# A hybrid encoder block on one core: the first tile's norm weights folded into its rounding, its high weight parts used first, and the last attention pair's reloads reordered

## The reference

```python
def _rmsnorm(x, g):
    y = xf * lax.rsqrt(jnp.mean(xf * xf, axis=-1, keepdims=True) + RMS_EPS)
    return (y * g)
...
h = _rmsnorm(x, norm_g)
proj = h @ w_in          # a_val, a_glu, z_a, q, k, v, z_b, g_logits
y_a = (_conv_module(a_val, a_glu, ...) * jax.nn.silu(z_a)) @ w_pw_a
attn = _neighbourhood_attention(q, k, v, rpb)   # 16 heads, 8 x 16 window, softmax
y_b = (attn * jax.nn.silu(z_b)) @ w_o_b
merged = sigmoid(g_a) * y_a + sigmoid(g_b) * y_b
out = _rmsnorm(x + merged @ w_out, final_g)
```

## Time and profile before

| | us |
|---|---|
| median of 3 runs | 1741.43 |
| lowest, highest | 1738.87, 1742.03 |
| the profiled execution's own time | 1739.94 |
| its span, first to last instruction | 1738.1 |

### The profile page before, as it was taken

How to read it: one execution, slowest core, us unless ns; L and a number is a source line. 1 busy time by engine, 2 the same in 40 slices (tenths; PEclk the granted TensorE clock), 3 DMA queues, 4 the chain that set the end, 5 groups by cost and what they waited for, 6 DMA issues and landing times.

```text
span 1738.1 us, 24594 instructions
## 1 busy us (share of the span) xinstructions
PE 1726.1 (99%) x8604; PEld 1405.8 (81%) x8604; DVE 1162.3 (67%) x1797; ACT 466.8 (27%) x925; POOL 200.2 (12%) x251
## 2 busy tenths in 40 slices
PE   9999999999999999999999999999999999999998
PEld 7888877788888888888888888888877888888886
DVE  6549255897689489579669948976985755335332
ACT  5411133123122122222222222221334344102222
POOL 1110011011011011101101100210110064000001
PEclk9999999999999999999999999999999999999999
DMA  8751345545435625634543453463467765543223
GB/s 296 244 93 49 94 110 142 157 121 158 127 86 168 169 50 145 173 84 125 167 126 97 133 164 90 121 167 111 115 171 282 256 208 175 192 133 110 74 91 127
DMA packets 299177, 247.56 MB, mean 142 GB/s; under 512 B 117815, under 2 KB 252999, under 8 KB 298988
## 3 DMA queue, kind: packets, MB, share of 16 engines
q1 hardware_dynamic: 246666, 153.04, 32.2%
q10 hardware_dynamic: 48578, 79.97, 13.3%
q0 software_dynamic: 3872, 13.75, 3.2%
HBM read 158.78 MB, written 87.90 MB: 142 GB/s over the span
## 4 chain that ended last, share of the span: by engine, by line
PE 89%; DMA 5%; DVE 2%; SPq 1%; ACT 1%; issue 1%; ACTq 0%; POOL 0%; POOLq 0%; DVEq 0%
PE pg L1523 71%; PE pg L1541 12%; PE pO L1638 3%; PE pS L1621 3%; DMA raw<-in_w_in 1%; DMA x_d<-work 1%; DMA work<-p_d 1%; DMA work<-tb_d 1%; SPq L528 1%; ACT xs L867 0%; DMA p_d<-work 0%; SPq L464 0%; DMA c_d<-work 0%; DVE work L1298 0%; ACT work L764 0%
## 5 line engine op out<-in xcount | busy, mean ns | idle before, releaser
L1523 PE MATMUL pg<-xs,ws 128*128 128x512 f32 x5688 | 1312.0, 391 | 0.8 <-DVE work L1419 0.5
L1523 PEld LDWEIGHTS pg<-xs,ws 128*128 128x128 f32 x5688 | 1062.1, 188 | 232.9 <-issue 11.4
L1214 DVE SCALAR_TENSOR_TENSOR work<-work 128x1551 f32<-128x1551 f32 x240 | 438.5, 1827 | 4.6
L1541 PE MATMUL pg<-ws,xs 128*128 128x512 f32 x1008 | 237.0, 393 | 0.7 <-DVE xs L1157 0.7
L1541 PEld LDWEIGHTS pg<-ws,xs 128*128 128x128 f32 x1008 | 190.4, 189 | 41.6 <-DVE ws L1108 1.0
L680 POOL TENSOR_TENSOR work<-work 128x384 f32<-128x384 bf16 (+1 forms) x72 | 62.3, 866 | 981.1 <-DVE small L1286 968.3
L1286 DVE CUSTOM_DVE_ANT_0 work<-pS,work 128x384 f32<-128x384 f32 (+1 forms) x192 | 88.4, 510 | 114.7 <-PE pS L1621 113.9
L955 ACT ACTIVATE work<-work,small 128x384 f32<-128x384 f32 (+1 forms) x192 | 109.2, 570 | 156.0 <-DVE small L1286 156.0
L1108 DVE TENSOR_TENSOR ws<-raw,ws 128x1024 fp32r<-128x1024 f32 x89 | 110.2, 1239 | 38.5 <-ACT ws L733 38.5
L733 ACT ACTIVATE ws<-raw 128x1024 fp32r<-128x1024 f32 x89 | 93.5, 1053 | 126.3 <-PE pg L1523 98.6
L1298 DVE STREAM_TRANSPOSE work<-work 128x384 f32<-128x384 f32 (+1 forms) x192 | 102.6, 534 | 6.6
(11 more groups left out here) (111 smaller groups left out, 905.8 us busy)
## 6 DMA issues: line engine op xcount, KB each, us to landing
raw<-in_w_in SPq DMA_DIRECT2D x70, 512.0 KB, 4.6
p_d<-work SPq DMA_DIRECT2D x256, 96.0 KB, 2.1
work<-p_d ACTq DMA_DIRECT2D x64, 384.0 KB, 5.1
work<-v_d SPq DMA_DIRECT2D x128, 96.0 KB, 2.7
p_d<-work SPq DMA_DIRECT2D x128, 64.0 KB, 1.9
work<-p_d ACTq DMA_DIRECT2D x32, 256.0 KB, 4.4
v_d<-work ACTq DMA_DIRECT2D x24, 256.0 KB, 2.1
za_d<-work ACTq DMA_DIRECT2D x24, 256.0 KB, 2.1
```

The source lines that it names most:

```text
L1214: nc.vector.scalar_tensor_tensor(cv[:, 0:CLEN], u[:, k:k + CLEN], cur[:, k:k + 1], cv[:, 0:CLEN], ALU.mult, ALU.add).then_inc(tap_ok, 1)
L1523: last = nc.tensor.matmul(pg[b][:], wt(s, wpart)[:, k * P:(k + 1) * P], xs[:, k, xpart, chunk(n)], start=(k == 0 and wpart == 1), stop=(k ...
L1541: last = nc.tensor.matmul(pg[b][:], xs[:, k, xpart, t * P:(t + 1) * P], wt(s0 + k // 2, wpart)[:, chunk(k % 2)], start=(k == 0 and xpart = ...
```

## The change

In the head the norm's weights of tile 0 are no longer multiplied into the row. PE turns them into a column by eight one-column transposes, DVE copies it to SBUF (`gcol`), and ACT's rounding and DVE's rest of tile 0 take it as a scale per partition, now in pieces of 128 columns. PE's first two groups are written out: the high weight parts of a slot are used by both parts of x before its low part is wanted, the next tile's transposes stand between, and group 1 begins before group 0 ends. Small products of the identity (`warm`) stand ahead and between the column's transposes. The rest of weight slot 0 moves from DVE to POOL. The squares of tiles 2 to 5 are placed otherwise. The broadcast of the norm's weights is issued behind weight slots 2 and 3.

In the last pair SP waits for the last probabilities before it issues tb tile 3, every tb tile has a semaphore, slot S_YB+1 is issued behind tile 6 and ahead of 0 and 1, and the refill of the first 512 tokens (and PE's first group on them) goes in the order 3, 4, 5, 2, 6, 7, 0, 1.

```diff
@@ -96,6 +96,7 @@
 EARLY = 11
+TB_ORDER = (3, 4, 5, 2, 6, 7, 0, 1)
 SHUFFLED = 5
...
@@ -448,9 +454,9 @@
             load_x(1)
-            sp.dma_start(ngb, norm_g[0:1, :].to_broadcast([P, D])).then_inc(ng_in, 16)
             for s in range(2, 4):
                 piece_s(s, w_rows(w0, C_V * P, s))
+            sp.dma_start(ngb, norm_g[0:1, :].to_broadcast([P, D])).then_inc(ng_in, 16)
             for t in range(2, 8):
...
@@ -528,12 +534,14 @@
             def load_tb(k):
-                sp.dma_start(home(k), tb_d[k]).then_inc(tbs_in, 16)
+                sp.dma_start(home(k), tb_d[k]).then_inc(tbs_in[k], 16)
             def load_tb_early():
                 sp.wait_ge(tb_out, 16 * (PAIRS - 1))
                 sp.wait_ge(qk_done, BLK * PAIRS)
+                for n in range(2):
+                    sp.wait_ge(p_in[n], 96 * PAIRS)
                 load_tb(3)
...
@@ -576,9 +584,6 @@
-            piece_y(S_YB + 1)
-            for n in range(2):
-                sp.wait_ge(p_in[n], 96 * PAIRS)
             sp.wait_ge(bias_ok, 18 * PAIRS)
...
@@ -586,6 +591,7 @@
             load_tb(6)
+            piece_y(S_YB + 1)
             sp.wait_ge(pv_done, BLOCKS * PAIRS)
...
@@ -646,11 +652,14 @@
             nc.gpsimd.memset(half, -0.5).then_inc(const_ok, 1)
-            nc.gpsimd.memset(onerow, 1.0).then_inc(const_ok, 1)
-            pool.wait_ge(const_ok, 3)
+            pool.wait_ge(const_ok, 2)
             nc.gpsimd.affine_select(out=ident[:], in_=ident[:], compare_op=ALU.not_equal, fill=1.0, base=0,
                                     pattern=[[-1, P]], channel_multiplier=1).then_inc(const_ok, 1)
             for t in range(NT):
+                if t == 1:
+                    pool.wait_ge(w_hi, 1)
+                    nc.gpsimd.tensor_tensor(wt(0, 1), raw_of(0), wt(0, 0).bitcast(F32), ALU.subtract).then_inc(w_lo, 1)
...
@@ -769,6 +778,13 @@
                     act.wait_ge(ht_ps, 2 * t + hf + 1)
+                if t == 0:
+                    act.wait_ge(gc_ok, 1)
+                    for k in range(4 * hf, 4 * hf + 4):
+                        nc.scalar.activation(xs[:, k, 0, 0:P], pH[k // 2][:, k % 2 * P:(k % 2 + 1) * P], ACT.Copy,
+                                             scale=gcol[:, k:k + 1]).then_inc(x_hi if k % 4 == 3 else x0_hi, 1)
+                    return
                 nc.scalar.activation(split_of(xs[:, 4 * hf:4 * hf + 4, 0, t * P:(t + 1) * P]), h_of(t, hf),
...
@@ -798,12 +814,19 @@
             for t in range(NT):
-                for n in range(t + (2 if t < 2 else 4), min(t + (3 if t < 1 else 5), NT)):
-                    square(n)
+                if t == 1:
+                    square(3)
+                    square(4)
+                elif t >= 2 and t + 4 < NT:
+                    square(t + 4)
                 if t + 1 < NT:
                     for hf in range(2):
                         h_hi(t + 1, hf)
+                    if t == 0:
+                        square(2)
                     take_v(t)
+                    if t == 1:
+                        square(5)
                 if t == 4:
...
@@ -857,7 +880,12 @@
                 act.wait_ge(g_done, g_next - NCH + n + 1)
-                for k in ks:
+                for k in TB_ORDER if (phase, n) == (1, 0) else ks:
+                    if phase == 1 and n == 0:
+                        if k == KT - 1:
+                            act.wait_ge(o_out, NCH * PAIRS)
+                        else:
+                            act.wait_ge(tbs_in[k], 16)
                     if phase == 2:
...
@@ -867,9 +895,6 @@
             def refill_tb(n):
-                if n == 0:
-                    act.wait_ge(tbs_in, 16 * 7)
-                    act.wait_ge(o_out, NCH * PAIRS)
                 refill_hi(1, n, lambda k: home(k)[:, chunk(n)], 1.0)
...
@@ -1128,9 +1153,8 @@
                     for hf in range(2):
-                        dve.wait_ge(ng_ps, hf + 1)
                         x = xt[:, 0, chunk(hf)]
-                        nc.vector.scalar_tensor_tensor(x, x, rstd[:, 0:1], pS[hf][:], ALU.mult, ALU.mult).then_inc(xn_ok, 1)
+                        nc.vector.tensor_scalar(x, x, rstd[:, 0:1], None, ALU.mult).then_inc(xn_ok, 1)
                     return
...
@@ -1152,16 +1176,26 @@
             def h_lo(t, hf):
+                if t == 0:
+                    for k in range(4 * hf, 4 * hf + 4):
+                        dve.wait_ge(*first_part(x_hi, x0_hi, k | 1))
+                        nc.vector.scalar_tensor_tensor(xs[:, k, 1, 0:P], pH[k // 2][:, k % 2 * P:(k % 2 + 1) * P],
+                                                       gcol[:, k:k + 1], xs[:, k, 0, 0:P].bitcast(F32), ALU.mult,
+                                                       ALU.subtract).then_inc(x_lo if k % 4 == 3 else x0_lo, 1)
+                    return
                 dve.wait_ge(x_hi, 2 * t + hf + 1)
                 rows = slice(4 * hf, 4 * hf + 4)
                 nc.vector.tensor_tensor(split_of(xs[:, rows, 1, t * P:(t + 1) * P]), h_of(t, hf),
                                         split_of(xs[:, rows, 0, t * P:(t + 1) * P].bitcast(F32)),
                                         ALU.subtract).then_inc(x_lo, 1)
+            dve.wait_ge(gc_ps, 1)
+            nc.vector.tensor_copy(gcol, pS[0][:, 0:KT]).then_inc(gc_ok, 1)
             mean_square_x(0)
             normalise(0)
-            split_s(0)
+            dve.wait_ge(gc_ok, 1)
             h_lo(0, 0)
+            dve.wait_ge(w_lo, 1)
             split_s(1)
...
@@ -1169,10 +1203,17 @@
             for t in range(1, NT):
-                for n in range(t + (1 if t < 3 else 3), min(t + (2 if t < 2 else 4), NT)):
-                    mean_square_x(n)
+                if t == 2:
+                    mean_square_x(3)
+                    mean_square_x(4)
+                elif t >= 3 and t + 3 < NT:
+                    mean_square_x(t + 3)
                 for hf in range(2):
                     h_lo(t, hf)
+                if t == 1:
+                    mean_square_x(2)
+                if t == 2:
+                    mean_square_x(5)
                 if t + 1 < SHUFFLED:
...
@@ -1516,13 +1557,15 @@
-                for k in range(4 * hf, 4 * hf + 4):
+                order = TB_ORDER if ready == 24 else range(KT)
+                for j in range(4 * hf, 4 * hf + 4):
+                    k = order[j]
                     if ready is not None:
-                        pe.wait_ge(x_lo, ready + k + 1)
+                        pe.wait_ge(x_lo, ready + j + 1)
                     for wpart, xpart in PASSES:
                         last = nc.tensor.matmul(pg[b][:], wt(s, wpart)[:, k * P:(k + 1) * P],
-                                                xs[:, k, xpart, chunk(n)], start=(k == 0 and wpart == 1),
-                                                stop=(k == KT - 1 and (wpart, xpart) == (0, 0)))
+                                                xs[:, k, xpart, chunk(n)], start=(j == 0 and wpart == 1),
+                                                stop=(j == KT - 1 and (wpart, xpart) == (0, 0)))
                 return last
...
@@ -1550,13 +1593,66 @@
                     pe.wait_ge(xn_ok, t + 2 if t else hf + 1)
-                    if 2 * t + hf >= 4:
+                    if t == 1:
+                        pe.wait_ge(x_lo, 2)
+                    elif t:
                         pe.wait_ge(x_lo, 2 * t + hf - 3)
                     for k in range(4):
-                        last = nc.tensor.transpose(pH[(2 * t + hf) % 4][:, k * P:(k + 1) * P],
+                        spot = pH[2 * hf + k // 2][:, k % 2 * P:(k % 2 + 1) * P] if t == 0 else (
+                            pH[(2 * t + hf) % 4][:, k * P:(k + 1) * P])
+                        last = nc.tensor.transpose(spot,
                                                    xt[:, t % 8, (4 * hf + k) * P:(4 * hf + k + 1) * P], ident[:])
                     last.then_inc(ht_ps, 1)
+            def warm(n):
+                for _ in range(n):
+                    nc.tensor.matmul(pg[1][:, 0:P], ident[:], ident[:], start=True, stop=True)
+            def first_groups():
+                def passes(t, ks, xpart, wpart):
+                    for k in ks:
+                        if t == 0 and wpart == 0:
+                            pe.wait_ge(*first_part(*((x_lo, x0_lo) if xpart else (x_hi, x0_hi)), k))
+                        last = nc.tensor.matmul(pg[t][:], xs[:, k, xpart, t * P:(t + 1) * P],
+                                                wt(k // 2, wpart)[:, chunk(k % 2)],
+                                                start=(k, xpart, wpart) == (0, 0, 0),
+                                                stop=(k, xpart, wpart) == (KT - 1, 0, 1))
+                    return last
+                def by_hi(s):
+                    pe.wait_ge(w_hi, s + 1)
+                    passes(0, (2 * s, 2 * s + 1), 0, 0)
+                    passes(0, (2 * s, 2 * s + 1), 1, 0)
+                def by_lo(s):
+                    pe.wait_ge(w_lo, s + 1)
```

(38 more changed lines are left out.)

15 lines of the change are left out of this document (9 added, 6 removed).

## The result

The changed kernel takes 1749.11 us (median of 6 runs, 1747.56 to 1751.03), the kernel before 1740.86 beside it (6 runs, 1738.87 to 1743.12); the ratio on record is 1.0036, 95% interval 1.0023 to 1.0050 (the quotient of the two medians is 1.0047, inside that interval). All times and ratios are of fast runs; three executions of the kernel before, of 1908 to 4448 us, are left out. Forecast was 1740.9, 1737.3 to 1744.3, with 0.09 for slower. The profiled execution took 1751.03 us (span 1749.2, mean clock 0.998), the slowest of the six; before's took 1739.94 (1738.1).

The account below looks back on a forecast made before the run. PE was taken as the bound, busy 1726.1 of 1738.1 us. Head +0.7 and last pair -1.2 gave -0.5 on the profiled 1739.94, so 1739.4; with 1.5 for the runs' median, 1740.9, range 1737.3 to 1744.3.

Parts of the forecast that it names:

- The transposes at 7.3 to 7.47: Head: PE's transposes of tile 0 start at 7.3 to 7.47 us, unchanged until 1/rms if the column is ready.
- POOL blocks DVE: Rival, head: POOL's subtraction holds up DVE's second half of tile 0; head +2.0 us, total 1742.2; chance 0.15.
- PE waits for its third slot until 13.5 to 13.9: Head: PE's first group starts at 9.3, then waits for ACT's split of slot 2, going on at 13.5 to 13.9 us.
- the clock stays low: Rival, head: small products don't raise PE's clock, group 1 ends about 1 us later; total 1741.9; chance 0.08.
- Tile 3 scaled at 26.9, the turn ends at 36.2: Head, DVE: tile 3 scaled at 26.9, 0.7 us later than before, so tile 6's turn ends at 36.2.
- By the row of shuffles L813 and the start at 99.89 move 0.7 us later.: Head to gate: seven shuffles of some 5.6 us each pass the turn's delay on; head +0.7 us, from +0.2 to +1.3.
- PE waits 1.7 us for L813: Gate: PE waits about 1.7 us for ACT's take, from 0.7 lead left, 0.7 shift and 0.3 from before.
- The last pair, -1.2: Last pair: waits for probabilities go, refill ends at 1330.7, 1.2 us earlier; at most 1.54 to gain.
- the slot: Last pair: slot S_YB+1 lands at 1324 (1323.3 to 1325), and ACT waits 3 to 4 us for it.
- +0.7 - 1.2: Sum of the forecast: head +0.7 us, last pair -1.2 us, together -0.5 us.
- The rivals at 1742.2 and 1744.9: 1742.2: POOL holds up DVE in the head, chance 0.15. 1744.9: S_YB+1 lands late in the last pair, chance 0.08.
- a lead of PE in the head is lost at the gate: Head: PE's 1.5 us lead is lost at the gate's start, 99.89, unless DVE ends tile 6's turn earlier.

Follow-up runs that it names:

- e3: The changed kernel with POOL's subtraction for weight slot 0 held until DVE has scaled both halves of tile 0; 1746.2 us, ratio 1.0018 to the kernel before.
- e12: The changed kernel with POOL's subtraction behind both scaled halves and the column's copy behind the scaling, tile 5's square left moved; 1747.2 us, ratio 1.0028.
- e4: The changed kernel with POOL's subtraction and the column's copy behind the scaling, and tile 5's square back with those of 3 and 4; 1740.2 us, ratio 0.9984.
- e14: The kernel before with only tile 5's square, and its mean on DVE, moved as in the changed kernel; 1747.8 us, ratio 1.0026.
- e13: The changed kernel with only tile 5's square and its mean moved back to those of tiles 3 and 4; 1744.3 us, ratio 1.0014.
- e1: The kernel before with only the last pair's part of the change, head untouched; 1744.4 us, ratio 1.0010.
- e9: The kernel before with ACT's split of weight slot 8 moved behind the second take of the V accumulator; 1739.6 us, ratio 0.9984.

## Why the prediction was wrong, step by step

**The transposes at 7.3 to 7.47.** Measured: 10.21. Two things were missed. I let nothing change "as long as the column is ready", but the column's copy stands ahead of the first mean square on DVE and waits for PE; e3, without the block, still starts at 8.08. And POOL blocks DVE, held as a rival at 0.15, with the wrong half and 0.7 to 2 us: the argument that DVE's instruction is queued first was false by 0.06 us: POOL's subtraction stands behind its own 1/rms of tile 0 and starts at 7.54, not 7.05, just ahead of DVE's first half. This case's rows now show what the Trainium skill, SBUF — State Buffer, section "SBUF: two separate sides", says, that the shared ports are held for a whole instruction by whoever starts first: 2559 ns beside POOL's 2.34 us, 474 behind it, 0.88 for both with POOL later (e3). By that rule PE starts later by what the first half took longer, 2559 - 474 = 2.09 us; e3 against the changed kernel gives 10.21 - 8.08 = 2.13.

**PE waits for its third slot until 13.5 to 13.9.** Right where the start was right: 13.79 in e12 and e4, and in e12 group 1 ends at 24.52, forecast 24.3 to 24.7. The rival "the clock stays low" is out: tile 1's transposes took 1.04 us (18.02 us in the changed kernel), where those at half clock took 1.97.

**Tile 3 scaled at 26.9, the turn ends at 36.2.** In e12, which has the head as I assumed it, 26.87 and 36.83. Of the 0.6 between, 0.44 are DVE's wait for POOL's 1/rms, whose mean is asked for just ahead of it. So the size of this step was nearly right.

**"By the row of shuffles L813 and the start at 99.89 move 0.7 us later."** This is the step that failed. At the turn 4.0 us had come where 0.7 was forecast, 2.7 by the transposes' late start and 1.3 by the square; another 4.5 came in the row of shuffles, where nothing was forecast. I measured the row's seven shuffles once, divided and took their time as fixed. It is not: 1.7 us at the turn became 8.9 at the last read-back in e14, 1.3 became 5.4 in e12, while 2.1 at the turn became 3.2 in e13, where PE's groups moved along. The row was fast before because the stores lay between the writes. I never set the stores' times against the writes'. The row also scatters by itself (33.6 to 36.7 us with before's head), which one measurement could not show.

**PE waits 1.7 us for L813.** 2.86, in e12 1.68. Not priced was what such a wait costs after it: half clock for over 3 us, 1.6 us.

**The last pair, -1.2.** The slot, set by the delay of 10.5 back to before's time, landed at 1325.4 (1321.40 + 14.52 - 10.50), forecast 1324; the refill's end by the same reckoning 1332.0, forecast 1330.7. ACT stood idle ahead of the slot for 6.42 us, forecast 3 to 4. The place was right and the size 1.3 off, so -1.2 became +0.2 in the changed kernel, +0.8 in e4 and +1.7 in e1.

Together: where +0.7 - 1.2 stood, the profile has +10.5 and +0.2. By ratios: e14's step alone +0.26%, e13's rest of the change +0.14%, the changed kernel +0.36%. The rivals at 1742.2 and 1744.9 named places that did lose time, POOL's block and the slot, but none had the row. That a lead of PE in the head is lost at the gate was right: in e12 PE's second V store goes out 1.4 us earlier than before, and the gate starts 4.9 later.

## What to carry to other kernels

A row of store-and-read-back steps has no fixed pace. Before moving its start against another stream of stores, put the issue times of both side by side; a shift by 1.6 us of one against the other cost more here (e14, 1747.8) than a shift of both by 2.1 (e13, 1744.3). On an in-order engine place a small input of a critical row (here a square) ahead of the evacuation that waits for PE, and a copy that waits for another engine behind it. And look at what stands behind a split that waits for a late load: one such line moved gained 0.16% (e9), where the whole change lost 0.36%.
